# Gated linear attention in a three-block model: tables made inside the projection's stage, and a chunk loop with both directions on the two halves of the array

## What is computed

```
q, k = heads(gq) * 128**-0.5, heads(gk);  v = heads(gv)
la_f = log_sigmoid(glr_f @ w2_f + b_f) / 16      # and la_b likewise
o = gla_chunked(q, k, v, la_f) + rev(gla_chunked(rev(q), rev(k), rev(v), rev(la_b)))
o_a = rms_norm(o) * silu(gr)

def gla_chunked(q, k, v, log_a):                 # per chunk of 64 tokens
    cum = cumsum(log_a);  q_dec = q * exp(cum);  k_inv = k * exp(-cum)
    scores = where(causal, q_dec @ k_inv.T, 0)
    k_tail = k * exp(cum_last - cum);  chunk_kv = k_tail.T @ v
    state' = exp(cum_last) * state + chunk_kv    # goes from chunk to chunk
    return scores @ v + q_dec @ state
```

## Time and profile before

| what | value |
|---|---|
| runs shown | 5344.79, 5377.94, 5491.37 us, median 5377.94 |
| the profiled execution | 5307.42 us, span 5305.6 us |
| PE / DVE / ACT / POOL busy | 72% / 37% / 20% / 17% of the span |
| mean granted TensorE clock | 0.838 |
| the four stages above | 3147.7 to 3255, to 3411, to 3662.3 us, and `join_mix` about 4285 to 4500 us |

### The profile page before, as it was taken

How to read it: one execution, slowest core, us unless ns; L and a number is a source line. 1 busy time by engine, 2 the same in 40 slices (tenths; PEclk the granted TensorE clock), 3 DMA queues, 4 the chain that set the end, 5 groups by cost and what they waited for, 6 DMA issues and landing times. The chain is left out here.

```text
span 5305.6 us, 63105 instructions
## 1 busy us (share of the span) xinstructions
PE 3798.9 (72%) x24826; PEld 2922.7 (55%) x24826; DVE 1967.5 (37%) x2433; ACT 1065.0 (20%) x1560; POOL 898.1 (17%) x626
## 2 busy tenths in 40 slices
PE   3797884838769997468997886495399920748992
PEld 1796444837535554357996764242388820636661
DVE  5213446061446664231105552423344457221112
ACT  0111222110313332110111223312123232101121
POOL 0001230000234442000002100000244434011002
PEclk7898885959879998789998997698699965859996
DMA  6322003232642211332212222454544333249984
GB/s 235 102 73 76 6 20 118 79 133 74 222 92 60 60 38 72 135 115 84 96 61 91 67 68 72 124 124 129 180 116 119 99 137 147 106 147 367 323 293 174
DMA packets 392620, 641.09 MB, mean 121 GB/s; under 512 B 97437, under 2 KB 253725, under 8 KB 387933
## 3 DMA queue, kind: packets, MB, share of 16 engines
q1 hardware_dynamic: 373978, 587.47, 34.3%
q10 hardware_dynamic: 10880, 25.17, 1.6%
q0 software_dynamic: 7568, 25.70, 1.3%
HBM read 451.17 MB, written 187.09 MB: 120 GB/s over the span
## 5 line engine op out<-in xcount | busy, mean ns | idle before, releaser
L455 PE MATMUL in_ps_p<-in_wh,h 128*128 128x352 f32 (+1 forms) x1600 | 363.1, 314 | 21.5 <-DVE in_wl L468 21.5
L455 PE MATMUL out_ps_p<-out_wh,m 128*128 128x256 f32 (+1 forms) x1152 | 279.8, 336 | 54.2 <-DVE out_wl L468 54.2
L455 PEld LDWEIGHTS in_ps_p<-in_wh,h 128*128 128x128 f32 x1600 | 273.4, 191 | 22.3 <-DVE in_wl L468 12.7
L455 PE MATMUL rest__ps_p<-rest__wh,h 128*128 128x388 f32 x1024 | 265.5, 340 | 15.5 <-DVE rest__wl L468 15.5
L1822 PE MATMUL cg_ps_p<-h,cg_wh 128*128 128x512 f32 x768 | 247.5, 404 | 14.2 <-POOL cg_wl L1801 14.2
L1594 PE MATMUL la_ps_s<-la_q,la_k 104*128 104x512 f32 x960 | 254.1, 400 | 2.5 <-DVE la_q L1674 2.5
L3213 PE MATMUL ex_ps_g<-ex_wgu,ex_xt 128*128 128x256 f32 x1024 | 234.7, 388 | 27.0 <-ACT ex_xt L3247 13.3
L455 PE MATMUL in_ps_p<-in_wl,h 128*128 128x352 f32 (+1 forms) x800 | 250.9, 314 | 0.0
L1632 ACT ACTIVATE la_pt<-la_ps_s 128x1024 f32<-128x1024 f32 x160 | 163.7, 1023 | 399.8 <-PE la_ps_s L1594 399.8
L455 PEld LDWEIGHTS out_ps_p<-out_wh,m 128*128 128x128 f32 x1152 | 200.6, 194 | 76.7 <-issue 46.5
L1549 POOL TENSOR_TENSOR la_accp<-la_accp,la_pt 128x1024 f32<-128x1024 f32 x80 | 195.0, 2438 | 229.4 <-ACT la_pt L1632 229.4
(11 more groups left out here) (580 smaller groups left out, 7574.5 us busy)
## 6 DMA issues: line engine op xcount, KB each, us to landing
ex_wgu<-in_moe_w_gate_dram SPq DMA_DIRECT2D x32, 1024.0 KB, 8.2
ex_wgu<-in_moe_w_up_dram SPq DMA_DIRECT2D x32, 1024.0 KB, 10.7
ex_wd<-in_moe_w_down_dram SPq DMA_DIRECT2D x32, 1024.0 KB, 9.7
ada_w<-in_w_ada_dram SPq DMA_DIRECT2D x12, 2048.0 KB, 18.1
dl_row<-rows SPq DMA_DIRECT2D x32, 512.0 KB, 4.7
yb<-ex_y SPq DMA_DIRECT2D x32, 512.0 KB, 6.3
p<-in_o SPq DMA_DIRECT2D x8, 1760.0 KB, 7.2
rest__w<-in_w_in_dram SPq DMA_DIRECT2D x16, 776.0 KB, 8.1
```

Source lines behind the costliest of these rows:

```text
L455: mm = te.matmul(ps[n % NB][:, 0:cw], a, b, start=k == 0 and n_ == 0, stop=k == kt - 1 and n_ == 2)
```

## The change

Two new functions take the place of three, and `join_mix` takes one GLA tensor in place of two.

`gla_tables` (tiles `gt_`) does the projection, the tables and the masked scores in one stage. It runs 8 units, each a head and a half of the tokens (512). For each, TensorE makes `z` for both directions, the q projection, the scores and transposed tail keys of the unit before, and the k projection. Nothing of q and k goes to DRAM: VectorE multiplies straight out of PSUM. The gate's bias is now a 33rd row of the weight. The tail keys are the inverse keys times the chunk decay. The decayed q (`gla_q`), the decays (`gla_d`) and the masked scores (`gla_s`) stay on chip; for each chunk the masked scores of the two directions are added, since both multiply the same values. Only `kl` goes to DRAM.

`gla_chunks` (tiles `gl_`) is written out step by step, 16 steps. The forward chunk lies on partitions 0 to 63 and the backward one on 64 to 127. The summed scores are used in the first 8 steps only; the results of these steps are kept on chip (`part`), and in the last 8 steps GpSimd adds them, so that one summed output is stored. The state lies in two buffers.

```
+def gla_tables(nc, ident, h_t, w, w_lr, w2, b2, resets, keep, qd, sm, de, kl):
...
+            @block.tensor
+            def _(te):
...
+                for u, (h, hf) in enumerate(units):
+                    for d in both:
...
+                        te.matmul(pz[d][:], wp[d][:, h * P:(h + 1) * P], lr_t[:, hf * HB:(hf + 1) * HB], start=True, stop=True).then_inc(*pe.did(f"z{d}_{u}"))
+                    project(0, u)
+                    if u:
+                        local(u - 1)
+                        te.wait_ge(*dve.at(f"qd1_{u - 1}"))
+                    project(1, u)
+                local(U - 1)
...
+def gla_chunks(nc, qd, sm, de, kl, v, out):
...
+                for c in range(NC):
+                    l, vv, o = lt[c % NB], vt[c % NB], po[c % 2]
+                    if c + 1 < NC:
+                        te.wait_ge(l_in[c % NB], 64 * (c // NB + 1))
+                        for g in both:
+                            if c:
+                                te.wait_ge(*dve.at(f"S{g}_{c - 1}"))
+                            for h in range(2 * g, 2 * g + 2):
+                                for d in both:
+                                    mm = te.matmul(pk[:, d, h, :], l[half[d], h * P:(h + 1) * P], vv[half[d], h * GV:(h + 1) * GV], start=True, stop=True)
+                            mm.then_inc(*pe.did(f"kv{g}_{c}"))
+                    if c >= 2:
+                        te.wait_ge(*act_s.at(f"p1_{c - 2}" if c - 2 < H2 else f"o_{c - 2}"))
+                    if c < H2:
+                        for h in range(GH):
+                            for d in both:
+                                mm = te.matmul(o[half[d], h, :], sm[half[d], h, chunk(c, d) % H2, :], vv[half[d], h * GV:(h + 1) * GV],
+                                               start=h % 2 == 0, stop=c == 0 and h % 2 == 1)
+                        mm.then_inc(*pe.did(f"in_{c}"))
+                    if c:
+                        te.wait_ge(*dve.at(f"S1_{c - 1}"))
+                        for h in range(GH):
+                            for d in both:
+                                t0 = chunk(c, d) * GC
+                                mm = te.matmul(o[half[d], h, :], qd[:, d, h, t0:t0 + GC], state[c % 2][:, d, h, :],
+                                               start=c >= H2 and h % 2 == 0, stop=h % 2 == 1)
+                        mm.then_inc(*pe.did(f"io_{c}"))
...
+                for c in range(NC):
+                    if c + NB - 1 < NC - 1:
+                        load(c + NB - 1)
+                    if c >= H2:
+                        sp.wait_ge(*pool.at(f"ad_{c}"))
+                        for d in both:
+                            t0 = chunk(c, d) * GC
+                            sp.dma_start(out[t0:t0 + GC, :], ot[c % 2][half[d], :]).then_inc(o_out[c % 2], 16)
...
-                        sp.dma_start(f[j][:], (gla, gdn)[x][0][rows, :]).then_inc(fb_in[j].sem, 16)
-                        sp.dma_start(b[j][:], (gla, gdn)[x][1][rows, :]).then_inc(fb_in[j].sem, 16)
+                        sp.dma_start(f[j][:], (gla, gdn[0])[x][rows, :]).then_inc(fb_in[j].sem, 16)
+                        if x:
+                            sp.dma_start(b[s][:], gdn[1][rows, :]).then_inc(fb_in[j].sem, 16)
```

More of the change, by code:

```diff
@@ L2040, in _, with load @@
-                run_ahead(sp, GH, load, store)
-                for d in range(2):
-                    sp.wait_ge(*out_[d].now(GH - 1))
+                def load(j, h):
+                    sp.dma_start(wt[j][:], w[:, j * GH * P + h * P:j * GH * P + (h + 1) * P].rearrange("(k p) n -> p k n", p=P)).then_inc(w_in[j], 16)
+                sp.dma_start(wr[:], w_lr.rearrange("(k p) n -> p k n", p=P)).then_inc(wr_in, 16)
+                for j in both:
+                    load(j, 0)
+                sp.wait_ge(zer, 2)
@@ L2084, in _ @@
+                give(U - 1)
             @block.vector
             def _(ve):
[L2086 to L2117 removed]
@@ L2169, in store, with load @@
-                def store(it, b):
-                    for d in range(2):
-                        c = place(sp, chunk(it, b, d) * GC, GC)
-                        sp.wait_ge(*act_s.now(it, f"o{d}{b}"))
-                        sp.dma_start(out[d][c, :], ot[d][b][:]).then_inc(out_[d][b].sem, 16)
-                run_ahead(sp, rounds, load, store)
-                for d in range(2):
-                    for b in range(2):
-                        sp.wait_ge(*out_[d][b].now(rounds - 1))
+                def load(c):
+                    if c >= NB:
+                        sp.wait_ge(*pe.at(done(c - NB)))
+                    for d in both:
+                        t0 = chunk(c, d) * GC
+                        sp.dma_start(lt[c % NB][half[d], :], kl[d][t0:t0 + GC, :]).then_inc(l_in[c % NB], 16)
+                        sp.dma_start(vt[c % NB][half[d], :], v[t0:t0 + GC, :]).then_inc(l_in[c % NB], 16)
@@ new lines, in _ @@
+            @block.scalar
+            def _(act):
+                for c in range(NC):
+                    act.wait_ge(*pe.at(last(c)))
+                    if c < H2:
+                        for d in both:
+                            act.activation(part[half[1 - d], H2 - 1 - c, :].rearrange("p (h n) -> p h n", h=GH), po[c % 2][half[d], :, :], ACT.Copy).then_inc(*act_s.did(f"p{d}_{c}"))
+                    else:
+                        if c >= H2 + 2:
+                            act.wait_ge(o_out[c % 2], 32 * ((c - H2) // 2))
+                        act.activation(ot[c % 2][:].rearrange("p (h n) -> p h n", h=GH), po[c % 2][:], ACT.Copy).then_inc(*act_s.did(f"o_{c}"))
@@ L2844, in join_mix @@
                        *[f"ev{k}{s}" for s in Z for k in range(2)])
-        pool = st.steps("pool", *each("ad"), *each("pw"), *each("gg"))
+        pool = st.steps("pool", *[f"ad{s}" for s in Z], *each("pw"), *each("gg"))
         pe = st.steps("pe", "tr0", "tr1")
```

538 lines of the change are left out of this document (245 added, 293 removed).

## The result

The changed kernel takes 5037.8 us (median of 4 runs, 5023.2 to 5041.8). The kernel before, run beside it, takes 5361.4 us (4 runs, 5344.8 to 5491.4). The ratio is 0.940, with a 95% interval of 0.935 to 0.945: faster, and inside the range. The forecast of 5103 us was 65 us too high.

The account below looks back on a forecast made before the run. TensorE bounds projection and loop, a chain through engines the tables. 514.6 - 151 - 99 + 10 = 275 us saved: 5032 from the profiled 5307.4, 5103 against the median 5377.9. Range 5020 to 5190, the forecast's own 5050 to 5165.

Parts of the forecast that it names:

- The sum: Whole kernel: old GLA part 514.6 us less new tables, loop and join saving gives 275 us saved, 5032 profiled.
- the last term: Whole kernel: profiled execution was 1.3% faster than the median of runs, so 5032 us was raised to 5103.
- The table stage: Projection with tables: eight units of 15.6 us set by TensorE, plus start and end, 151 us in all.
- the price of ScalarE's chain: Table stage: ScalarE's passes, table loads, copies and a wait take 13.3 us a unit, hidden under TensorE's 15.6.
- The loop: Chunk loop: 38 phases of 1.95 us with overlapping halves, plus ends, late loads and low clock, 99 us, from 251.
- The late loads: Chunk loop, second half: loads issued behind stores arrive late, lengthening three steps by 3 us, 7 in all.
- The forecast's check of bandwidth: Chunk loop: 1.28 MB a step in 4.9 us needs 260 GB/s, which holds because the join moves 410.
- The join: `join_mix`: two of 16 loads fewer a round, 1.3 us each over four rounds, saves 10 us.
- Turns between the halves: Rival, chunk loop and tables: halves do not overlap, a phase takes 4.0 us, kernel 5198 us; 5%.
- Turns for the scores alone: Rival, chunk loop: only score products take turns, eight phases grow by 2.05, 16 us, kernel 5119 us; 4%.
- A drain at each change of half: Rival, loop and tables: each record costs its whole duration; at 0.50 us a record the kernel takes 5438 us; 2%.
- The low clock in the changed kernel's loop: Rival, chunk loop: clock stays at 1.2 GHz, PE takes 74 us more, less 10 already counted, kernel 5167 us; 6%.

Follow-up runs that it names:

- e11: Kernel before with only a comment added, profiled once more: its chunk loop took 278.1 us, against 257.0 in a second such execution.
- e3_before_grouped: Kernel before with each direction's four state products placed ahead of its four score products: median 5281.0 us, loop 231.2 against 256.9.
- e2_loads_first: Changed kernel with a step's stores in the last eight steps issued one step later, behind the next loads: loop 94.2 us.
- e5_no_ln: Changed kernel with the gate table's logarithm replaced by an exponential, so ScalarE reloads no function table in the units: table stage 156.2 us, as before the edit.
- e6_two_passes: Changed kernel with two of three passes in the q and k projections, 16 matmuls fewer a unit: unit 12.44 us, stage 131.4.
- e4_join_two: Changed kernel with the join loading the GLA output twice and adding the copies, 16 loads a round again: join 207.0 us against 194.0.
- e9_one_half: Changed kernel with both directions of the chunk loop on one half of the array: phases 3.6 us, loop 166.8 us.
- e8_two_queues: Changed kernel with the loop's value loads issued by ScalarE, and SyncE keeping key loads and late stores: loop 94.2 us, median 5026.6.
- e1_turns: Changed kernel with head and direction loops swapped, forward half's matmuls first, then the backward half's (two heads at a time in key products): loop 117.9 us.
- e10_again: Changed kernel unchanged, timed again beside more runs of the kernel before: ratio 0.937, median 5026.6 us, loop 96.8 us.

## Why the forecast was right, and where it was off

**The sum held, the last term did not.** The profiled executions differ by 273.4 us, where the sum said 275, and 5034.0 us was measured against 5032. The mechanisms are the forecast's, but that close an agreement is partly luck: the tables came out 5.2 us too long and the loop 1.8, and the join's 3.7 and the 2 us by which the untouched stages differ made up for most of it. The step that failed is the one in the last sentence of the sum: to add 71 us because the profiled execution of before was 1.3% faster than the median of its runs. By it the time lies below the forecast's own range of 5050 to 5165, in the part that was added for the case in which "the runs come out like the profiled one", as they did. The changed kernel has no such gap. Its eight runs lie within 5019 to 5042 us and its profiled ones, 5034.0 and 5024.4, among them. The spread of before belongs at least in part to the stage that the change replaces: in e11 all of the 21 us are in the old loop, and e3_before_grouped, with the same loop in another order, lies within 5264 to 5293 in nine runs. So 71 us should not have been carried over in full, and the middle of the range should have stood near 5032. The run of 6269.9 us with e2_loads_first warns that the changed kernel may not be free of such spread either.

**The table stage** (151 forecast, 156.2 measured). Gate product 1.9 (1.8), scores 0.98 (1.1), tail keys 1.85 (1.8), 48 matmuls at 0.2265 the same: their sum is 15.6, but the unit is 16.07. The missing term is about 0.1 us at each change of form among them, 0.46 a unit and 3.7 in eight. The rest is in the last unit: PE waited 2.89 us for VectorE, as forecast, but the clock then fell, and the last tail keys took 3.6 us in place of 1.9. The low bound for the scores (1.0) was nearer than the value taken. That TensorE sets the unit is shown by e5_no_ln and e6_two_passes; the price of ScalarE's chain was wrong in size but not in sign.

**The loop** (99, 100.8). Phases are 1.88 and 1.93, not 1.95, and a step of the second half takes 3.81, not 3.95: 2.3 us less over all steps. VectorE is nearly level with PE there, as said. Its eight updates take 3.22 us, and its idle time falls from 2.46 us in the first half to 0.58:

```profile
3358.53 3.22 DVE L2254 SCALAR_TENSOR_TENSOR gl_S<-gl_S,gla_d,gl_ps_k 128x256 f32<-128x256 f32 x8 [2.46 <-PE gl_ps_k L2203]
...
3368.02 3.22 DVE L2254 SCALAR_TENSOR_TENSOR gl_S<-gl_S,gla_d,gl_ps_k 128x256 f32<-128x256 f32 x8 [0.58 <-PE gl_ps_k L2203]
```

The late loads were named with their place (every third step after the eighth) and size (3; measured 3.61 and 4.07, 7.7 for the forecast's 7). Their issue was underpriced, 2.9 us for four and not 1.8. The clock was given 3 us and took 6.4: 2.3 at the start (the first key phase 3.71 and score phase 2.41) and 4.1 behind the two waits (1.8 and 0.8 in the two phases behind the first, 1.0 and 0.5 behind the second), which the sum had not linked to the clock. That gives 99 - 2.3 + 0.7 + 3.4 = 100.8. The forecast's check of bandwidth, 260 GB/s against the join's 410, allowed too much: in this loop the DMA engines are full at 250 to 290 GB/s.

**The join** (10, 13.7). The cause is as said: e4_join_two gives the time back by its two loads a round. The term was eight loads at 1.3. A load is 1.28 us within a round, but 13.0 to 13.7 us is 1.6 to 1.7 for each of the eight; the rest falls between the rounds and was not looked into.

**The rivals.** Turns between the halves would have been 3.6 us a phase and 66 us in the loop (e9_one_half), where the sum had 71 (78 less 7) for it. Turns for the scores alone didn't happen: 1.88 us. A drain at each change of half didn't happen either: a phase changes half with every matmul and takes 1.88 us, 0.12 a record. The low clock in the changed kernel's loop is seen for a few us at its start and behind the waits; in e9_one_half it lasted until about 3352, 32 us after PE's first record, so the same start can take longer.

Three things stay open: what the runs of before near 5475 us spend their time on, why the loop's transfers fill the DMA engines at a lower rate than the join's, and whether e2_loads_first or e8_two_queues is faster than the changed kernel at all. Each shortens the profiled loop to 94 us, but the medians, 5019.6 and 5026.6 against 5026.6 and 5037.8, are from different chips or too close.

## What to carry to other kernels

Work that runs as a chain through the small engines cost nothing here once it stood unit by unit beside a long run of matmuls, because each engine's sum per unit stayed below TensorE's; count every change of matmul form at about 0.1 us. Two independent streams with 64 rows or 64 columns each belong on the two halves of the array, matmul by matmul in turn, for nearly twice the speed. Check bandwidth against transfers of the same shape: the busy share of the DMA engines tells, not the bytes alone. Forecast from one profiled execution to the same one, and carry the gap to the median over only if it lies in stages that the change keeps.

## What the runs showed of the hardware

- Of 32-bit matmuls with 256 columns each half of the array takes a record every 0.216 us, and with the halves in groups of eight the second half starts three records early (e1_turns). On one half they come every 0.225 us (e9_one_half).
- Where stationary operands of different shape alternate record pair by record pair, a record takes 0.287 us in place of 0.234 (e3_before_grouped).
- The granted clock of one program's loop rose at about 3420, 3421 and 3476 us in three executions (from the means 0.88, 0.87 and 0.67 of their windows); in the last, PE was busy 98% of the 40 us window in which it rose. In the changed kernel's loop it fell once within a wait of 3.61 us and once just behind one of 4.07; with a wait of 3.85 us in another execution it did not (e10_again).
- Back to back, a load onto 64 partitions occupies SyncE's queue for 0.60 us and more.
- The 16 DMA engines are full at 415 GB/s in the join (share 1.02) but at 252 to 294 GB/s in the chunk loop (shares 0.98 to 1.05), whose transfers touch 64 partitions each.
